# Four column strips for the Toeplitz kernels of a state-space layer: eight on-chip copies become thirty-two

## What is computed

```python
def s5_layer(h, ...):
    xn = rmsnorm(h, g_pre)
    u, z = jnp.split(xn @ w_in, 2, axis=-1)
    y = s5_ssm(u, a_re, a_im, log_dt, b_re, b_im, c_re, c_im, d_skip)
    y = jax.nn.gelu(y)
    ...
# s5_ssm, for each group of 16 channels:
#   h_t = Abar h_{t-1} + Bbar u_t ;  y_t = Re(C h_t) + D * u_t
```

## Time and profile before

| | |
|---|---|
| time, median of 3 runs | 3483.96 us (3482.14 to 3485.89) |
| time of the profiled execution | 3486.52 us |
| its span | 3484.7 us |
| TensorE clock granted, mean over the span | 0.964 of 2.4 GHz |
| TensorE matmul busy | 3246.0 us (93% of the span) |
| ScalarE, VectorE, GpSimd busy | 1145.8, 1435.7, 1619.3 us |
| stretch with Toeplitz copies | from 112.5 us to 535.2 us (starts of the first and last issue) |

### The profile page before, as it was taken

How to read it: one execution, slowest core, us unless ns; L and a number is a source line. 1 busy time by engine, 2 the same in 40 slices (tenths; PEclk the granted TensorE clock), 3 DMA queues, 4 the chain that set the end, 5 groups by cost and what they waited for, 6 DMA issues and landing times.

```text
span 3484.7 us, 48561 instructions
## 1 busy us (share of the span) xinstructions
PE 3246.0 (93%) x18540; PEld 2529.4 (73%) x18540; DVE 1435.7 (41%) x2229; ACT 1145.8 (33%) x1500; POOL 1619.3 (46%) x1292
## 2 busy tenths in 40 slices
PE   5799998999899999999989889999999999967797
PEld 4688886878668787878868757777777777734486
DVE  8777783120242222222230144444534534546512
ACT  4344442233333332322342333323223323315521
POOL 2566662444557667777744424344444434400142
PEclk9899998999999999999999999999999999978899
DMA  3555555232212222222212222222212212211222
GB/s 129 156 155 161 160 164 156 96 143 88 95 57 80 81 84 84 84 84 84 82 61 99 84 103 82 82 74 85 81 71 73 89 68 83 79 57 48 92 92 94
DMA packets 117903, 332.97 MB, mean 96 GB/s; under 512 B 58512, under 2 KB 61712, under 8 KB 86544
## 3 DMA queue, kind: packets, MB, share of 16 engines
q1 hardware_dynamic: 117776, 331.08, 28.2%
HBM read 296.96 MB, written 29.36 MB: 94 GB/s over the span
## 4 chain that ended last, share of the span: by engine, by line
PE 73%; issue 16%; POOL 5%; DVE 4%; ACT 1%; DMA 0%; ACTq 0%; SPq 0%; POOLq 0%; DVEq 0%
PE bank L159 21%; PE bank L161 20%; PE bank L160 20%; POOL wlo L146 4%; PE bank L1308 2%; PE bank L1014 1%; PE bank L1032 1%; PE bank L422 1%; ACT whi L140 1%; PE bank L421 1%; PE bank L433 1%; PE bank L407 1%; PE bank L1023 0%; PE bank L999 0%; PE bank L1288 0%
## 5 line engine op out<-in xcount | busy, mean ns | idle before, releaser
L146 POOL TENSOR_TENSOR wlo<-wraw,whi 128x512 fp32r<-128x512 f32 x912 | 1245.3, 1397 | 1685.9 <-ACT whi L140 1685.8
L159 PE MATMUL bank<-rhi,whi 128*128 128x512 f32 x3648 | 1494.2, 410 | 108.3 <-POOL wlo L146 37.5
L160 PE MATMUL bank<-rlo,whi 128*128 128x512 f32 x3648 | 1433.8, 393 | 0.0
L161 PE MATMUL bank<-rhi,wlo 128*128 128x512 f32 x3648 | 1433.7, 393 | 0.0
L159 PEld LDWEIGHTS bank<-rhi,whi 128*128 128x128 f32 x3648 | 691.8, 190 | 326.2 <-issue 92.7
L161 PEld LDWEIGHTS bank<-rhi,wlo 128*128 128x128 f32 x3648 | 691.8, 190 | 148.9
L160 PEld LDWEIGHTS bank<-rlo,whi 128*128 128x128 f32 x3648 | 693.3, 190 | 140.9 <-issue 11.3
L140 ACT ACTIVATE whi<-wraw 128x2048 fp32r<-128x2048 f32 x228 | 437.0, 1917 | 617.9 <-PE bank L161 471.0
L845 POOL TENSOR_TENSOR wraw<-wraw,vec 128x512 f32<-128x512 f32 x260 | 266.3, 1056 | 0.0
L753 DVE TENSOR_TENSOR ssum<-ssum,wk 128x512 f32<-128x512 f32 x30 | 21.6, 719 | 311.4 <-ACT wk L743 311.4
L743 ACT ACTIVATE wk<-bank 128x512 f32<-128x512 f32 x32 | 27.8, 870 | 236.7 <-PE bank L161 236.7
(11 more groups left out here) (351 smaller groups left out, 3252.5 us busy)
## 6 DMA issues: line engine op xcount, KB each, us to landing
wraw<-in_wall_dram SPq DMA_DIRECT2D x228, 1024.0 KB, 4.8
g<-in_bmat_dram SPq DMA_DIRECT2D x16, 512.0 KB, 5.4
g<-scr_e SPq DMA_DIRECT2D x128, 64.0 KB, 4.8
scr_a<-ssum SPq DMA_DIRECT2D x32, 256.0 KB, 2.1
g<-in_xp_dram SPq DMA_DIRECT2D x4, 1024.0 KB, 11.7
g<-in_cmat_dram SPq DMA_DIRECT2D x16, 256.0 KB, 4.5
scr_u<-wk SPq DMA_DIRECT2D x16, 256.0 KB, 5.9
scr_y<-wk SPq DMA_DIRECT2D x16, 256.0 KB, 2.2
```

The source lines that it names most:

```text
L146: ins = pool.tensor_tensor(wlo[:, slot, c], wraw[:, slot, c], whi[:, slot, c].bitcast(F32), ALU.subtract)
L159: pe.matmul(acc[slot][:, :], whk, rhi[:, k, :], start=(k == 0), stop=False)
L160: pe.matmul(acc[slot][:, :], whk, rlo[:, k, :], start=False, stop=False)
L161: ins = pe.matmul(acc[slot][:, :], wlk, rhi[:, k, :], start=False, stop=(k == KT - 1))
```

## The change

The K matmuls of the eight groups no longer all write partitions 0 to 15 of two PSUM banks. Group g writes partitions 32(g mod 4) to 32(g mod 4)+15 of one bank, at columns 128(g div 4), so four groups stand in four column strips of the array. `kst` becomes 128 partitions x 256 columns (16 rows used in each strip of 32; the rest is zeroed once by GpSimd). ScalarE copies it in four pieces of 16x256. The D table takes the same layout. A Toeplitz copy now reaches from one strip to one block row of `tt`, for the two groups of that strip, so there are 4 x 8 = 32 copies a step.

```diff
-                kv = m["kst"][0:SC, :].rearrange("c (g n) -> c g n", g=GT)
-                tv = m["tt"].rearrange("p (g n) -> p g n", g=GT)
+                kv = m["kst"].rearrange("c (g n) -> c g n", g=2)
+                tv = m["tt"].rearrange("p (g q n) -> p g q n", g=2, q=4)
                 for s in range(L):
-                    sp.dma_start(tv[s * SC:(s + 1) * SC, :, s * SC:P], kv[:, :, 0:P - s * SC]).then_inc(t_in, 16)
+                    for q in range(4):
+                        sp.dma_start(tv[s * SC:(s + 1) * SC, :, q, s * SC:P], kv[32 * q:32 * q + SC, :, 0:P - s * SC])\
+                          .then_inc(t_in, 16)
...
-                sp.dma_start(m["dk"][0:SC, :], a["dk"][j]).then_inc(dk_in, 16)
+                sp.dma_start(m["dk"], a["dk"][j]).then_inc(dk_in, 16)
...
-                k0 = m["kst"][0:SC, :].rearrange("c (g n) -> c g n", g=GT)[:, :, 0:SC]
-                d.tensor_tensor(k0, k0, m["dk"][0:SC, :].rearrange("c (g n) -> c g n", g=GT),
-                                ALU.add).then_inc(k_rdy, 1)
+                k0 = m["kst"].rearrange("c (g n) -> c g n", g=2)[:, :, 0:SC]
+                d.tensor_tensor(k0, k0, m["dk"].rearrange("c (g n) -> c g n", g=2), ALU.add).then_inc(k_rdy, 1)
...
                 for g in range(GT):
-                    ins = pe.matmul(ps_k[g // 4][0:SC, (g % 4) * P:(g % 4 + 1) * P], m["bb"][:, g * SC:(g + 1) * SC],
+                    q = 32 * (g % 4)
+                    ins = pe.matmul(ps_k[q:q + SC, g // 4 * P:(g // 4 + 1) * P], m["bb"][:, g * SC:(g + 1) * SC],
                                     q1[v][:, g * 144:g * 144 + P], start=True, stop=True)
...
-                for i in range(2):
-                    act.activation(m["kst"][0:SC, i * 512:(i + 1) * 512], ps_k[i][0:SC, :], ACT.Copy).then_inc(k_cp, 1)
+                for q in range(4):
+                    rows = slice(32 * q, 32 * q + SC)
+                    act.activation(m["kst"][rows, :], ps_k[rows, 0:2 * P], ACT.Copy).then_inc(k_cp, 1)
...
+            pool.memset(m["kst"], 0.0)
             pool.memset(m["tt"], 0.0).then_inc(t_zero, 1)
```

More of the change, by code:

```diff
@@ L182, in program @@
         m |= cut(g2, [("pr", SG * 9), ("pi", SG * 9), ("crq", SG), ("ciq", SG), ("r8", SG), ("m8", SG),
-                      ("p", GT * P), ("bt", 1024), ("et", 1024), ("tt", 1024), ("cq", 512), ("bb", 128), ("dk", 128)])
+                      ("p", GT * P), ("bt", 1024), ("et", 1024), ("tt", 1024), ("cq", 512), ("bb", 128), ("dk", 32)])
         m |= cut(g1, [("q1a", 1152), ("q1b", 1152), ("cosa", 512), ("cosb", 512),
                       ("sina", 512), ("sinb", 512), ("m8a", 512), ("m8b", 512), ("uga", 512)])
-        m |= cut(wk, [("ta", 1152), ("kst", 1024), ("ua", 512), ("ub", 512), ("ugb", 512), ("ph", 512),
+        m |= cut(wk, [("ta", 1152), ("kst", 256), ("", 768), ("ua", 512), ("ub", 512), ("ugb", 512), ("ph", 512),
                       ("t1", 512), ("t2", 512), ("hs", 512), ("yg", 512), ("kk", NCH)])
@@ L201, in program @@
         cq4 = m["cq"].rearrange("q (i g c) -> q i g c", i=4, g=GT)
-        ps_x, ps_y, ps_k, ps_st = banks[2], banks[4], banks[5:7], banks[7]
+        ps_x, ps_y, ps_k, ps_st = banks[2], banks[4], banks[5], banks[7]
         par_in = sem("par_in")
@@ L381, in dve_step @@
                 t = j - 1
-                d.wait_ge(k_cp, 2 * t + 2)
+                d.wait_ge(k_cp, 4 * t + 4)
                 d.wait_ge(dk_in, 16 * t + 16)
-                k0 = m["kst"][0:SC, :].rearrange("c (g n) -> c g n", g=GT)[:, :, 0:SC]
-                d.tensor_tensor(k0, k0, m["dk"][0:SC, :].rearrange("c (g n) -> c g n", g=GT),
-                                ALU.add).then_inc(k_rdy, 1)
+                k0 = m["kst"].rearrange("c (g n) -> c g n", g=2)[:, :, 0:SC]
+                d.tensor_tensor(k0, k0, m["dk"].rearrange("c (g n) -> c g n", g=2), ALU.add).then_inc(k_rdy, 1)
                 d.wait_ge(be_in, 16 * (L + 1) * t + 16 * (L + 1))
@@ L404, in pe_step @@
                 pe.wait_ge(q_rdy, t + 1)
-                wait(pe, k_cp, 2 * t)
+                wait(pe, k_cp, 4 * t)
                 for g in range(GT):
-                    ins = pe.matmul(ps_k[g // 4][0:SC, (g % 4) * P:(g % 4 + 1) * P], m["bb"][:, g * SC:(g + 1) * SC],
+                    q = 32 * (g % 4)
+                    ins = pe.matmul(ps_k[q:q + SC, g // 4 * P:(g // 4 + 1) * P], m["bb"][:, g * SC:(g + 1) * SC],
                                     q1[v][:, g * 144:g * 144 + P], start=True, stop=True)
@@ L414, in pe_step @@
                 pe.wait_ge(hcs, t + 1)
-                pe.wait_ge(t_in, P * t + P)
+                pe.wait_ge(t_in, 4 * P * t + 4 * P)
                 wait(pe, yg_rdy, t)
@@ L453, in act_step @@
                 act.wait_ge(k_mm, t + 1)
-                wait(act, t_in, P * t)
-                for i in range(2):
-                    act.activation(m["kst"][0:SC, i * 512:(i + 1) * 512], ps_k[i][0:SC, :], ACT.Copy).then_inc(k_cp, 1)
+                wait(act, t_in, 4 * P * t)
+                for q in range(4):
+                    rows = slice(32 * q, 32 * q + SC)
+                    act.activation(m["kst"][rows, :], ps_k[rows, 0:2 * P], ACT.Copy).then_inc(k_cp, 1)
                 act.wait_ge(ph_rdy, t + 1)
@@ L2133, in lay_out @@
     out["kn"] = np.broadcast_to(np.arange(NCH), (P, NCH)).astype(np.float32)
-    dk = np.zeros((KT, SC, GT, SC), np.float32)
-    dk[:, np.arange(SC), :, np.arange(SC)] = np.asarray(i["s5_d"])[0].reshape(KT, GT, SC).transpose(2, 0, 1)
-    out["dk"] = dk.reshape(KT, SC, GT * SC)
+    dk = np.zeros((KT, 4, 32, 2, SC), np.float32)
+    dk[:, :, np.arange(SC), :, np.arange(SC)] = np.asarray(i["s5_d"])[0].reshape(KT, 2, 4, SC).transpose(3, 0, 2, 1)
+    out["dk"] = dk.reshape(KT, P, 2 * SC)
     return {k: np.ascontiguousarray(v, dtype=np.float32) for k, v in out.items()}
```

## The result

| | before | after |
|---|---|---|
| time, median of 4 runs | 3484.93 us | 3603.88 us (3601.82 to 3606.48) |
| time of the profiled execution | 3486.52 us | 3605.18 us |
| span | 3484.7 us | 3603.4 us |
| clock granted, mean | 0.964 | 0.946 |
| 15 steps between first Toeplitz copies | 418.2 us | 532.0 us |

The ratio is 1.0336, with a 95% interval of 1.0323 to 1.0348: 119.0 us slower. The forecast was +114.8 us. Of the 118.7 us by which the span grew, 532.0 - 418.2 = 113.8 us lie between the first and the last set of copies.

A forecast was written before the change was run, and what follows sets the result against it. TensorE bounds the kernel before; SyncE's issues would set the pace after. 110.4 (fifteen steps) + 4.2 (end) + 0.2 (GpSimd's clearing) = +114.8 us on 3484.0 gives 3599 us, range 3570 to 3635.

The forecast's parts named there:

- The price of an issue: On SyncE, 0.649 us from one Toeplitz copy to the next; 24 more copies add 15.6 us a step.
- The rival of cheap issues: Copies issue on SyncE 0.37 us apart and the strips pay: 3476 us; chance 0.10.
- The slack: SyncE's waits over 15 steps, 106.4 us for Y matmuls, 15.5 for GpSimd, 1.3 for `q1`: 123.2 us, shrinking to nothing.
- The sum: Over the 15 steps between sets of copies: 15 x 15.6 - 123.2 = +110.4 us.
- the wait for the store of u: SyncE's wait for u to land before loading it back: 85.2 us, no slack, unchanged.
- The steady step: Each of ten steps goes from 29.29 to 35.7 us, with SyncE setting the pace.
- The end: Last Y matmuls start when the copies land, 21.9 us after the last first copy, not 17.7: +4.2 us.
- Strips: K matmuls on TensorE gain 0 to 1.37 us a step if strips overlap, worth nothing at SyncE's pace.
- The clock: Rival: TensorE's clock falls after waits and TensorE becomes the bound, about 3625 us; chance 0.11.
- ScalarE: Two evacuations become four of half the length: at most +1.2 us a step, hidden because copies wait for SyncE.
- two waits in a steady step: TensorE idles before the X matmuls and before the Y matmuls, 6 to 8 us a step.

The follow-up runs named there:

- micro: Kernel before plus eleven forms of single transfers after its last output, on a quiet core: issues 0.59 to 0.62 us SBUF to SBUF, 0.31 to 0.47 with HBM.
- dram32: Changed kernel, but the Toeplitz source is first stored to HBM and the 32 copies read it from there: 3658.16 us, ratio 1.05.
- micro2: Kernel before plus HBM-to-SBUF transfers after its last output, on a quiet core, rows 1 KB or 2 KB apart: issues went from 0.59 to 0.42 us.
- dram32p: As dram32, but the scratch rows in HBM lie 2 KB apart, not 1 KB: 3562.36 us, ratio 1.0221 to the kernel before.
- s8: Kernel before with K matmuls in four strips, which ScalarE gathers onto 16 partitions, so eight Toeplitz copies stay: 3475.01 us, ratio 0.9968.
- s16: As s8, but each Toeplitz copy is cut in two, 16 issues a step, same bytes: 3474.26 us, ratio 0.9974 to the kernel before.
- s24: As s8, but each Toeplitz copy is cut in three, 24 issues a step, same bytes: 3524.44 us, ratio 1.0111 to the kernel before.
- act16: Changed kernel, but ScalarE's queue issues the 16 copies of strips 2 and 3, SyncE the other 16: 3482.9 us, ratio 0.9985 to the kernel before.
- early_u: Changed kernel, but SyncE stores u before the previous step's tables and loads it back behind them: 3543.44 us, ratio 1.0163 to the kernel before.

## Why the prediction was right

**The price of an issue** was right (0.649 us from one to the next; 0.646 measured, the mean over the sixteen sets), **the reason only in part.** "What sets the 0.60 us is neither size nor the number of pieces" holds over micro's five forms. "That both ends lie in SBUF, the one thing that only L298 has, does" is true as far as it goes, since all six forms with an end in HBM were cheaper, but it is not the one thing: dram32 and micro2 have issues of 0.56 to 0.59 us with the source in HBM. The sum took no harm from it: the new copies have both ends in SBUF, and that alone kept every form of micro at 0.59 to 0.62. The rival of cheap issues reckoned with 0.37 us and turned to a loss at about 0.41; even dram32p's 0.478 would not have brought it.

**The slack** of 123.2 us was used up as said. s8, s16 and s24 show where: with 8 copies the Y wait is 97.4 us, with 16 it is 31.6, with 24 none.

**The sum.** Predicted were 234 - 123.2 = +110.4 us for the fifteen steps (15.58 us each). Measured: 24 x 0.646 x 15 = 232.6, less 123.2, plus 3.2 by which the wait for the store of u grew, is 112.6 of the 113.8 seen. I had called that wait unchanged; it is a transfer's landing, and it moved a little. The steady step was 35.8 us in the mean (35.7 predicted): 35.3 to 35.9 in seven of the ten, and 36.1, 36.5 and 37.4 in the others.

**The end.** The last Y matmuls start at 666.61, 22.4 us after the last first copy, where it was 17.7: +4.6 us (4.2 predicted). The profile puts that wait of 12.6 us down to no releaser ("issue"); that it ends with the landing of the copies fits the times (last issue at 664.8, 1.8 us to land). The time before and behind the fifteen steps grew by 118.7 - 113.8 = 4.9 us, the start of this among it.

**Strips** overlap (0.63 us for sixteen records), which was left open, and are worth nothing at SyncE's pace, as said; s8 shows their worth where TensorE bounds, 1.3 us a steady step of the 1.37 at most (from the last matmul before the K matmuls to the first behind them it is 0.88 us, where it was 2.17).

**The clock** fell after waits, as the rival had it, but TensorE had time to give. Of a step of 35.8 us it is busy for 31.6, slow matmuls included. At full clock its work takes 28.0 (s8), so of the 7.8 us that it had to give, 3.6 went to the slower clock and 4.2 to standing still. act16 bears on this: without SyncE's pace its two-tile steps are back at 28.0 us.

**ScalarE.** Four evacuations at 0.376 us are 1.5 us against 1.16: +0.35 (at most 1.2 predicted), hidden. early_u shows that the cover is thin: with SyncE 3.6 us a step faster, k_rdy becomes what SyncE waits for.

**Named wrong:** where TensorE waits, and for what. I had two waits in a steady step, before the X and before the Y matmuls, together 6 to 8 us. There is one, before the X matmuls, and TensorE stands still for 4.2 us: by the time it reaches the Y matmuls the copies have landed. For that wait I had named the last table and P from VectorE; in the steady steps the profile names the load of u (4.08 us in the timeline above), and P mostly when u comes early (32.2 us in 14 waits in early_u; 5.2 in 2 waits after the change, in one-tile steps). All of these are late because SyncE is, so the sum did not suffer.

**The version to keep** is s8: strips for the matmuls, brought together by ScalarE on the way out of PSUM, where the shape is free to change. It is 10 us (0.3%) faster than the kernel before and 129 us faster than the one after; s16 is no slower.

## What to carry to other kernels

Count the transfers that one queue issues in a step, not only their bytes: what a queue has left in a step is the time in which it waits for other engines, and once that is used up, each further transfer costs its full issue time at every step (77.5 us here from 24 to 32 copies). When a layout that suits TensorE multiplies transfers, change the layout back in the evacuation, which cost a fraction of a microsecond a step here, or share the issues between two queues. And when a rate is the bound, look at what differs between two kinds of step: if light and heavy steps take the same time (34 to 35 and 35.8 us here), the pace is not set by the engine whose load differs.

## What the runs showed of the hardware

- Four fp32 matmuls with 16 weight columns, in strips at partitions 0, 32, 64 and 96, ran fully side by side: sixteen records in 0.63 us, each as long as before (273 ns), in fours with starts some 7 ns apart. From the last matmul before them to the first behind them it was 0.88 us in place of 2.17; the edges to the matmuls with 128 weight columns cost no more than before the change.
- The time to issue a transfer depended on its ends and hardly on its size: 0.59 to 0.62 us from SBUF to SBUF for 16 to 256 pieces, 0.31 to 0.47 us with HBM at one end, and 0.56 to 0.59 from HBM when 32 pieces at an even distance went to 16 partitions of two. Moving HBM rows from 1 KB to 2 KB apart brought the last to 0.42. All of this is from SyncE's queue; an SBUF-to-SBUF issue on ScalarE's took 0.615 us.
- In a row of four cheap issues the first took 0.31 to 0.34 us and the others some 0.42 (0.39 and 0.47 with two pieces on each of 128 partitions), and in a row of sixteen the others stayed at 0.42; in dram32p their median was 0.373.
